# Expert weights in rows of 16 KB: pairs of slots filled by one transfer, and the transposes that match

## The chip, the cores and the metric

The kernel runs on one core of a Trainium2 chip. A core has a matrix engine (PE, TensorE), whose weight loads are shown apart as PEld, and VectorE (DVE), ScalarE (ACT), GpSimd (POOL) and SyncE (SP), each with an instruction stream of its own. They meet at semaphores. Sixteen DMA engines move data between HBM and the on-chip memory SBUF. The metric is the time of one execution on the device, in microseconds, lower is better.

## What is computed

One layer of a hybrid diffusion backbone on 512 latent and 128 context tokens of width 2048, in f32: gated linear attention and windowed attention side by side, a merge, and then the part that matters here, a mixture of 16 experts in which each expert chooses its tokens (64 latent and 16 context ones, 80 rows).

```python
gate, idx = lax.top_k(aff.T, cap)
xs = xf[idx]                                             # 80 rows of 2048
hid = silu(einsum('ecd,edf->ecf', xs, w_gate)) * einsum('ecd,edf->ecf', xs, w_up)
ye = einsum('ecf,efd->ecd', hid, w_down) * gate[..., None]
y = zeros_like(xf).at[idx.reshape(-1)].add(ye.reshape(-1, D))
```

`w_gate` and `w_up` are 2048 x 1024 per expert and `w_down` is 1024 x 2048, 8 MB each: 24 MB per expert, 384 MB in all, each used once.

## The kernel before

The stages up to the router fill the first 60% of the time. After them runs a loop over the experts, with its last round written out because the output work lies in it.

**Pieces and slots.** The weights of an expert come in 24 pieces of 1 MB (128 partitions x 2048 values, 8 KB in each partition): pieces 0 to 7 are `w_gate`, 8 to 15 `w_up`, 16 to 23 `w_down`. Piece j goes to slot j % 8 (`ESLOTS`). Slots 0 and 1 are two of the four slots of the buffer `ring`, slots 2 to 6 lie in `hT`, slot 7 in `ar`. SyncE issues the transfers (`expert`, L623) as each slot comes free: piece j waits until VectorE has finished piece j - 8 (`piece_ready`).

**From piece to product.** ScalarE copies a piece into its high part (fp32r, L1834) and VectorE subtracts to get the low part (L2323). Both lie in one of four split buffers (`SP`), which PE frees (`piece_used`). PE then does three products of high and low parts per tile: 12 matmuls of 512 columns for each piece (L1446 for gate and up, L1471 for down). The tokens are the stationary operand, 80 columns.

**Which row a partition holds.** A product sums over the partitions, so weights and tokens must put the same row of the contraction in the same partition. A gate or up piece covers 256 rows of 4 KB. Partition p gets rows 2p and 2p + 1 of them, 8 KB in one run of HBM. So the tokens' columns that PE transposes for it are every second one, `xs[:, 256 g + 2 p + k]` (L1420 to L1423): the 128 values that one transpose loads as its stationary operand stand 8 bytes apart. A down piece covers 128 rows of 8 KB, one in each partition, and the transposes of the hidden rows (L1430) read 128 adjacent columns.

**Order on PE.** After the 192 gate and up matmuls of an expert come four hidden transposes (L1430), twelve token transposes for the next expert (L1422, k = 0 to 11), four hidden ones, the first down piece, the last four token transposes (k = 12 to 15), and seven more down pieces. Before expert 0 stand sixteen token transposes in three groups, each behind a part of the norm (`norm_xs`, L2326, on VectorE). GpSimd gathers the tokens of the expert after next, adds finished rows into `y`, and in the last round loads and stores the blocks of `y`.

Of the kernel before, what the change touches and what calls it, by code (L numbers as in the profile page):

```python
# [22 lines left out]
ds = bass.ds  # L23

P = 128
D = 2048
# [165 lines left out]
def build(nc, T):  # L192
# [2 lines left out]
    w_a = T["w_branch_a"][0].rearrange("(k p) n -> p k n", p=P)  # L195
    w_b = T["w_branch_b"][0].rearrange("(k p) n -> p k n", p=P)
    w_out = T["w_out"][0].rearrange("(k p) n -> p k n", p=P)
    w_eg = T["w_exp_gate"][0].rearrange("e (g p k) n -> e g p k n", p=P, k=2)
    w_eu = T["w_exp_up"][0].rearrange("e (g p k) n -> e g p k n", p=P, k=2)
    w_ed = T["w_exp_down"][0].rearrange("e (k p) n -> e p k n", p=P)  # L200
    x_lat, x_ctx = T["x_sample"][0], T["x_prompt"][0]
    x_of = [x_lat[t * P:(t + 1) * P, :] for t in range(4)] + [x_ctx]
    x_out = [T["y_sample"][0], T["y_prompt"][0]]
# [10 lines left out]
    with ExitStack() as ctx:  # L214
# [357 lines left out]
        @block.sync  # L572
        def _(sync):
            def load(g, src, dst=None):

                first, turn = g
                s = first % SLOTS

                sync.wait_ge(slot_used, first + turn + 1)
                sync.sem_inc(loads_issued, 1)  # L580
                out = ring[:, s, :] if dst is None else dst(ring[:, s, :])
                sync.dma_start(out, src).then_inc(slot_ready[s], 16)

            def k4(v):
                return v.rearrange("p (k n) -> p k n", k=4)

            def k2(v):
                return v.rearrange("p (k n) -> p k n", k=2)

            for t in range(NT):  # L590
                sync.dma_start(xrow[:, t, :], x_of[t]).then_inc(x_ld[t], 16)
            for q in range(SECTIONS):
                for m in range(2):
                    for j in range(4):
                        cols = slice(m * D + q * BANK, m * D + (q + 1) * BANK)
                        load((G_MOD + 8 * q + 4 * m + j, 0), w_mod[:, 4 * j:4 * j + 4, cols], k4)
                    if m == 0:
                        sync.wait_ge(h_sq, q + 1)
                        sync.dma_start(k4(first_w[:, q, :]), w_in[:, 4 * q:4 * q + 4, 0:BANK]).then_inc(x_ld[q], 16)
            loaded = {"W": 0, "M": 0}  # L600
            for at, (kind, i) in enumerate(CHUNK_ORDER):
                block, j = loaded[kind] // 4, loaded[kind] % 4
                loaded[kind] += 1
                col = (0, BANK, 2 * BANK, 3 * BANK, COL_GR, COL_GR + BANK, COL_SKV, COL_SQ, COL_SQ + BANK)[i]
                if kind == "W":
                    load((G_A + at, 0), w_in[:, 4 * j:4 * j + 4, col:col + BANK], k4)
                else:
                    load((G_A + at, 0), w_mod[:, 4 * j:4 * j + 4, 2 * D + block * BANK:2 * D + (block + 1) * BANK], k4)
            with sync.Fori(0, 4) as n:
                for j in range(12):  # L610
                    w, at = (w_a, w_b)[j // 6], j % 6
                    if at < 4:
                        src = w_in[:, 4 * at:4 * at + 4, ds(n * BANK + (COL_GATE_A, COL_GATE_B)[j // 6], BANK)]
                    else:
                        src = w[:, 4 * (at - 4):4 * (at - 4) + 4, ds(n * BANK, BANK)]
                    load((G_GATE + gate_place(j), n * 24), src, k4)
                    cols = ds(n * BANK + 5 * D, BANK) if j >= 8 else ds(n * (2 * BANK) + (3 * D + j // 4 * BANK), BANK)
                    load((G_GATE + mod_place(j), n * 24), w_mod[:, 4 * (j % 4):4 * (j % 4) + 4, cols], k4)
            with sync.Fori(0, 4) as n:
                for j in range(4):  # L620
                    load((G_OUT + j, n * 4), w_out[:, 4 * j:4 * j + 4, ds(n * BANK, BANK)], k4)

            def expert(e, j):  # L623

                sync.wait_ge(piece_ready, e * EXP_G + (P_EXP + j + 1 - ESLOTS))
                sync.sem_inc(loads_issued, 1)
                at, out = ds(e, 1), exp_slot[j % ESLOTS]
                if j < 16:
                    src = (w_eg, w_eu)[j // 8][at, j % 8, :, :, :].squeeze(0)
                    sync.dma_start(k2(out), src).then_inc(exp_ready[j % ESLOTS], 16)  # L630
                else:
                    sync.dma_start(out, w_ed[at, :, j - 16, :].squeeze(0)).then_inc(exp_ready[j % ESLOTS], 16)

            sync.wait_ge(slot_used, SLOTS + G_OUT + 16)
            for j in range(2):
                expert(0, j)
            sync.wait_ge(piece_used, SP + P_EXP)
            for j in range(2, 5):
                expert(0, j)
            sync.wait_ge(x1_sc, 4 * NT)  # L640
            for j in range(5, 7):
                expert(0, j)
            sync.wait_ge(xs_ld, 16)
            with sync.Fori(0, NE - 1) as e:
                for j in range(7, EXP_G):
                    expert(e, j)
                for j in range(7):
                    expert(e + 1, j)
            for j in range(7, EXP_G):
                expert(NE - 1, j)  # L650


        @block.gpsimd
# [230 lines left out]
        def _(pe):  # L884
# [532 lines left out]

            def xs_transposes(lo, hi, done, bank=0):

                v = xs[0:CAP, 0:D].rearrange("r (g p k) -> r g k p", g=8, k=2)  # L1420
                for k in range(lo, hi):
                    mm = pe.transpose(ps[:, bank + k // 6, (k % 6) * CAP:(k % 6 + 1) * CAP], v[:, k // 2, k % 2, :],  # L1422
                                      ident[0:CAP, 0:CAP])  # L1423
                mm.then_inc(done, 1)

            def hid_transposes(half):

                for k in range(4):
                    col = (4 * half + k) * P
                    mm = pe.transpose(ps[:, 2 + half, k * CAP:(k + 1) * CAP], hid[0:CAP, col:col + P], ident[0:CAP, 0:CAP])  # L1430
                mm.then_inc(hd_tr, 1)

            pe.wait_ge(af_cp, 1)
# [63 lines left out]
        def _(act):  # L1497
# [330 lines left out]
            def split_expert(e, lo, hi):  # L1828

                for j in range(lo, hi):  # L1830
                    s = j % SP
                    act.wait_ge(exp_ready[j % ESLOTS], e * (16 * EXP_G // ESLOTS) + 16 * (j // ESLOTS + 1))
                    act.wait_ge(piece_used, e * EXP_G + (P_EXP + j + 1))
                    act.activation(spE[:, s, 0, :], exp_slot[j % ESLOTS], ACT.Copy).then_inc(piece_high, 1)  # L1834

# [60 lines left out]
        def _(dve):  # L1896
# [429 lines left out]
            def norm_xs(lo, hi):  # L2326
                v = xs[0:CAP, lo:hi]
                dve.scalar_tensor_tensor(v, v, xs[0:CAP, D:D + 1], arows[0:CAP, lo:hi], ALU.mult, ALU.add).then_inc(n2_h, 1)
# [2 lines left out]
            dve.wait_ge(ga_is, 1)  # L2331
            low_expert(0, 0, 2)
            dve.wait_ge(xs_ld, 16)
            norm_xs(0, 768)
            norm_xs(768, 1536)
            norm_xs(1536, D)
            dve.wait_ge(af_cp, 2)
            low_xs(first_xs_parts[:1]).then_inc(xs_l, 1)
# [114 lines left out]
```

## Time and profile before

| | us |
|---|---|
| median of 3 runs | 2909.85 (2909.76 to 2911.56) |
| the profiled execution | 2907.71 |
| its span, first to last instruction | 2905.7 |
| PE busy in it | 2783.0 |
| DVE busy | 2257.8 |
| ACT busy | 1607.0 |

The rows further down come from that one execution. Busy times of engines overlap, so they don't add up to the span; an engine's idle time costs something only where another waits for it.

### The profile page before, as it was taken

How to read it: one execution, taken by the hardware profiler on the slowest of the kernel's cores; microseconds unless marked ns; L12 is line 12 of the kernel's file. 1: busy time of each engine (PE TensorE's matmuls, PEld its weight loads, DVE VectorE, ACT ScalarE, POOL GpSimd, SP SyncE). 2: the span in 40 equal slices, each digit the busy share in tenths (PEclk: the TensorE clock that was granted, in tenths of full speed). 3: DMA queues.
4: the chain of work that ended last, by engine and by line, in shares of the span. 5: the costliest groups of instructions: out<-in, count | busy, mean ns of one | idle time of the engine just before them, and what ended most of it. 6: DMA issues, size and time to landing. Idle time of an engine off the chain costs nothing.

```text
span 2905.7 us, 38120 instructions
## 1 busy us (share of the span) xinstructions
PE 2783.0 (96%) x13699; PEld 2078.4 (72%) x13699; DVE 2257.8 (78%) x2691; ACT 1607.0 (55%) x1977; POOL 305.1 (10%) x206
## 2 busy tenths in 40 slices
PE   6899899999899999999999996999999999999996
PEld 4798658899568888888888884666666666666663
DVE  2465666678878878888775558999998999999987
ACT  4336334444764444434434445777777777777775
POOL 0000000000000000000013000111221112211121
PEclk9999899999999999999999998999999999999998
DMA  9842103333014454454464437999999999999996
GB/s 372 308 131 73 50 19 114 107 120 131 1 61 158 145 178 145 152 172 147 163 254 163 147 119 280 403 402 395 378 388 380 390 385 389 389 385 381 384 377 267
DMA packets 175083, 683.14 MB, mean 235 GB/s; under 512 B 14548, under 2 KB 14756, under 8 KB 119164
## 3 DMA queue, kind: packets, MB, share of 16 engines
q1 hardware_dynamic: 159504, 613.45, 55.8%
q0 software_dynamic: 13392, 67.79, 7.6%
q8 instruction: 76, 1.25, 0.2%
q10 hardware_dynamic: 2064, 0.26, 0.1%
q14 instruction: 47, 0.39, 0.0%
HBM read 649.88 MB, written 31.65 MB: 235 GB/s over the span
## 4 chain that ended last, share of the span: by engine, by line
PE 92%; DVE 4%; ACT 2%; issue 1%; DMA 1%; POOL 0%; DVEq 0%; POOLq 0%; ACTq 0%; SPq 0%
PE ps L960 40%; PE ps L1446 24%; PE ps L1471 12%; PE ps L979 5%; PE ps L986 3%; PE ps L1422 1%; PE ps L1099 1%; PE ps L1250 1%; PE ps L1239 1%; PE ps L1134 1%; PE ps L1220 1%; DMA ring<-w_mod 1%; PE ps L924 1%; DVE ar L2047 0%; ACT ar L490 0%
## 5 line engine op out<-in xcount | busy, mean ns | idle before, releaser
L960 PE MATMUL ps<-split_weights,split_tokens 128*128 128x512 f32 x5040 | 1160.4, 391 | 3.9 <-issue 2.9
L960 PEld LDWEIGHTS ps<-split_weights,split_tokens 128*128 128x128 f32 x5040 | 943.9, 188 | 211.6 <-issue 10.2
L1446 PE MATMUL ps<-split_experts,split_xsT 128*80 128x512 f32 x3072 | 708.9, 392 | 0.0
L531 ACT ACTIVATE split_weights<-ring 128x512 fp32r<-128x512 f32 x384 | 242.9, 633 | 721.7 <-PE ps L960 605.9
L1446 PEld LDWEIGHTS ps<-split_experts,split_xsT 128*80 128x80 f32 x3072 | 454.8, 148 | 251.4 <-issue 1.5
L2323 DVE TENSOR_TENSOR split_experts<-hT,split_experts 128x2048 fp32r<-128x2048 f32 x240 | 540.0, 2284 | 41.2 <-ACT split_experts L1834 41.2
L535 DVE TENSOR_TENSOR split_weights<-ring,split_weights 128x512 fp32r<-128x512 f32 x384 | 266.3, 694 | 362.4 <-ACT split_tokens L532 358.7
L1834 ACT ACTIVATE split_experts<-hT 128x2048 fp32r<-128x2048 f32 x240 | 459.9, 1922 | 123.7 <-PE ps L1446 87.0
L1471 PE MATMUL ps<-split_experts,split_hidT 128*80 128x512 f32 x1536 | 362.3, 395 | 1.6 <-DVE split_experts L2323 1.2
L1471 PEld LDWEIGHTS ps<-split_experts,split_hidT 128*80 128x80 f32 x1536 | 226.7, 149 | 124.4 <-issue 2.5
L2323 DVE TENSOR_TENSOR split_experts<-ring,split_experts 128x2048 fp32r<-128x2048 f32 x96 | 220.0, 2293 | 42.9 <-ACT split_experts L1834 41.9
L538 DVE TENSOR_TENSOR split_tokens<-hT,split_tokens 128x640 fp32r<-128x640 f32 x304 | 249.8, 822 | 0.0
L1834 ACT ACTIVATE split_experts<-ring 128x2048 fp32r<-128x2048 f32 x96 | 184.7, 1925 | 83.1 <-PE ps L1446 51.5
L532 ACT ACTIVATE split_tokens<-hT 128x640 fp32r<-128x640 f32 x304 | 219.9, 723 | 0.0
L424 DVE SCALAR_TENSOR_TENSOR cst<-ring,cond,cst 128x512 f32<-128x512 f32 x300 | 213.0, 745 | 0.6 <-DMA ring<-w_mod 0.6
L979 PE MATMUL ps<-split_tokens,split_weights 128*128 128x384 f32 x768 | 180.6, 344 | 9.6 <-DVE split_tokens L562 9.6
L979 PEld LDWEIGHTS ps<-split_tokens,split_weights 128*128 128x128 f32 x768 | 126.8, 191 | 20.6 <-DVE split_tokens L562 14.3
L986 PE MATMUL ps<-split_tokens,split_weights 128*128 128x256 f32 x768 | 134.9, 285 | 3.0 <-ACT ar L1671 1.8
L833 POOL DMA_INDIRECT y_rows<-ar,sidx x15 | 105.6, 7041 | 279.2 <-DVE ar L2425 262.0
L986 PEld LDWEIGHTS ps<-split_tokens,split_weights 128*128 128x128 f32 x768 | 124.5, 191 | 4.0 <-ACT ar L1671 2.1
L2323 DVE TENSOR_TENSOR split_experts<-ar,split_experts 128x2048 fp32r<-128x2048 f32 x48 | 109.9, 2290 | 13.4 <-ACT split_experts L1834 13.4
L1834 ACT ACTIVATE split_experts<-ar 128x2048 fp32r<-128x2048 f32 x48 | 92.1, 1919 | 31.0 <-PE ps L1446 19.1
(327 smaller groups left out, 2058.3 us busy)
## 6 DMA issues: line engine op xcount, KB each, us to landing
ring<-w_mod SPq DMA_DIRECT2D x96, 1024.0 KB, 5.4
hT<-w_exp_gate SPq DMA_DIRECT2D x80, 1024.0 KB, 7.1
hT<-w_exp_up SPq DMA_DIRECT2D x80, 1024.0 KB, 8.1
hT<-w_exp_down SPq DMA_DIRECT2D x80, 1024.0 KB, 7.8
ring<-w_in SPq DMA_DIRECT2D x64, 1024.0 KB, 5.1
ring<-w_exp_gate SPq DMA_DIRECT2D x32, 1024.0 KB, 7.5
ring<-w_exp_up SPq DMA_DIRECT2D x32, 1024.0 KB, 7.4
ring<-w_exp_down SPq DMA_DIRECT2D x32, 1024.0 KB, 9.9
```

Source lines behind the costliest of these rows:

```text
L424: dve.scalar_tensor_tensor(acc, v, c, acc, ALU.mult, ALU.add).then_inc(z_rd, 1)
L531: self.eng.activation(spW[:, s, 0, :], raw, ACT.Copy)
L532: self.eng.activation(spX[:, s, 0, :], (src[k] if type(src) is dict else src[:, k, :]), ACT.Copy).then_inc(piece_high, 1)
L535: a = self.eng.tensor_tensor(spW[:, s, 1, :], raw, spW[:, s, 0, :].bitcast(F32), ALU.subtract)
L538: self.eng.tensor_tensor(spX[:, s, 1, :], (src[k] if type(src) is dict else src[:, k, :]), spX[:, s, 0, :].bitcast(F32), ALU.subtract).the ...
L960: mm = pe.matmul(ps[:, b, :], spX[:, s, x, b * P:(b + 1) * P], spW[:, s, w, :], start=(k == 0 and x == w), stop=(k == n_k - 1 and x == 1))
L979: mm = pe.matmul(ps[:, c, 0:TA], spW[:, s, w, c * P:(c + 1) * P], spX[:, s, x, 0:TA], start=(k == 0 and x == w), stop=(k == KT - 1 and w = ...
L986: mm = pe.matmul(ps[:, 4 + c // 2, (c % 2) * TB:(c % 2 + 1) * TB], spW[:, s, w, c * P:(c + 1) * P], spX[:, s, x, TA:TOK], start=(k == 0 an ...
L1446: mm = pe.matmul(ps[0:CAP, bank + i, :], xsT[:, x, k, :], spE[:, s, w, col:col + BANK], start=(k == 0 and x == w), stop=(k == KT - 1 and x ...
L1471: return pe.matmul(ps[0:CAP, 4 + n, :], hidT[:, x, k, :], spE[:, (16 + k) % SP, w, n * BANK:(n + 1) * BANK], start=(k == 0 and x == w), st ...
L1834: act.activation(spE[:, s, 0, :], exp_slot[j % ESLOTS], ACT.Copy).then_inc(piece_high, 1)
L2323: dve.tensor_tensor(spE[:, s, 1, :], exp_slot[j % ESLOTS], spE[:, s, 0, :].bitcast(F32), ALU.subtract)\
```

## The change

Slots 0 and 1, 2 and 3, and 4 and 5 are filled in pairs by one transfer of 2 MB; slots 6 and 7 stay alone. In each partition a pair holds one run of 16 KB from HBM: four rows of `w_gate` or `w_up`, or two of `w_down`. The issue waits until the second slot of the pair is free, which is one piece later than the first piece's issue was, and both pieces are there when the one transfer has landed: ScalarE waits on the semaphore of the pair's first slot.

The rows in a partition are others now, so the columns transposed change with them. For k = 0 to 11 the token columns are every fourth one (16 bytes apart), for k = 12 to 15 every second one as before. For the hidden rows, the first six of eight transposes read every second column, the last two adjacent ones. The first group of token transposes before expert 0 needs columns up to 1024, and the three parts of the norm are cut at 1024 and 1536 instead of 768 and 1536. Numbers of matmuls, splits and bytes stay as they are.

```diff
--- before.py
+++ after.py
@@ -195,9 +195,9 @@
     w_a = T["w_branch_a"][0].rearrange("(k p) n -> p k n", p=P)
     w_b = T["w_branch_b"][0].rearrange("(k p) n -> p k n", p=P)
     w_out = T["w_out"][0].rearrange("(k p) n -> p k n", p=P)
-    w_eg = T["w_exp_gate"][0].rearrange("e (g p k) n -> e g p k n", p=P, k=2)
-    w_eu = T["w_exp_up"][0].rearrange("e (g p k) n -> e g p k n", p=P, k=2)
-    w_ed = T["w_exp_down"][0].rearrange("e (k p) n -> e p k n", p=P)
+    w_eg = T["w_exp_gate"][0]
+    w_eu = T["w_exp_up"][0]
+    w_ed = T["w_exp_down"][0]
     x_lat, x_ctx = T["x_sample"][0], T["x_prompt"][0]
     x_of = [x_lat[t * P:(t + 1) * P, :] for t in range(4)] + [x_ctx]
     x_out = [T["y_sample"][0], T["y_prompt"][0]]
@@ -622,32 +622,34 @@
 
             def expert(e, j):
 
-                sync.wait_ge(piece_ready, e * EXP_G + (P_EXP + j + 1 - ESLOTS))
+                sync.wait_ge(piece_ready, e * EXP_G + (P_EXP + j + (2 if j % ESLOTS < 6 else 1) - ESLOTS))
                 sync.sem_inc(loads_issued, 1)
-                at, out = ds(e, 1), exp_slot[j % ESLOTS]
-                if j < 16:
-                    src = (w_eg, w_eu)[j // 8][at, j % 8, :, :, :].squeeze(0)
-                    sync.dma_start(k2(out), src).then_inc(exp_ready[j % ESLOTS], 16)
-                else:
-                    sync.dma_start(out, w_ed[at, :, j - 16, :].squeeze(0)).then_inc(exp_ready[j % ESLOTS], 16)
+                at, slot = ds(e, 1), j % ESLOTS
+                two = slot < 6
+                assert not (two and slot % 2)
+                out = (ring[:, 0:2, :].rearrange("p s n -> p (s n)") if slot == 0 else hT_area((slot - 2) * SLOT, 2 * SLOT)) if two else exp_slot[slot]
+                w, rows, per = ((w_eg, w_eu)[j // 8], 2 * P, 2) if j < 16 else (w_ed, P, 1)
+                lo, n = slot * rows, 2 if two else 1
+                src = w[at, lo:lo + n * rows, :].squeeze(0).rearrange("(p k) n -> p k n", k=n * per)
+                sync.dma_start(out.rearrange("p (k n) -> p k n", k=n * per), src).then_inc(exp_ready[slot], 16)
 
             sync.wait_ge(slot_used, SLOTS + G_OUT + 16)
-            for j in range(2):
-                expert(0, j)
+            def experts(e, lo, hi):
+
+                for j in range(lo, hi):
+                    if j % ESLOTS not in (1, 3, 5):
+                        expert(e, j)
+
+            experts(0, 0, 2)
             sync.wait_ge(piece_used, SP + P_EXP)
-            for j in range(2, 5):
-                expert(0, j)
+            experts(0, 2, 4)
             sync.wait_ge(x1_sc, 4 * NT)
-            for j in range(5, 7):
-                expert(0, j)
+            experts(0, 4, 7)
             sync.wait_ge(xs_ld, 16)
             with sync.Fori(0, NE - 1) as e:
-                for j in range(7, EXP_G):
-                    expert(e, j)
-                for j in range(7):
-                    expert(e + 1, j)
-            for j in range(7, EXP_G):
-                expert(NE - 1, j)
+                experts(e, 7, EXP_G)
+                experts(e + 1, 0, 7)
+            experts(NE - 1, 7, EXP_G)
 
 
         @block.gpsimd
@@ -1417,17 +1419,21 @@
 
             def xs_transposes(lo, hi, done, bank=0):
 
-                v = xs[0:CAP, 0:D].rearrange("r (g p k) -> r g k p", g=8, k=2)
+                four = xs[0:CAP, 0:3 * 4 * P].rearrange("r (g p k) -> r g k p", g=3, k=4)
+                two = xs[0:CAP, 3 * 4 * P:D].rearrange("r (g p k) -> r g k p", g=2, k=2)
                 for k in range(lo, hi):
-                    mm = pe.transpose(ps[:, bank + k // 6, (k % 6) * CAP:(k % 6 + 1) * CAP], v[:, k // 2, k % 2, :],
+                    column = four[:, k // 4, k % 4, :] if k < 12 else two[:, k // 2 - 6, k % 2, :]
+                    mm = pe.transpose(ps[:, bank + k // 6, (k % 6) * CAP:(k % 6 + 1) * CAP], column,
                                       ident[0:CAP, 0:CAP])
                 mm.then_inc(done, 1)
 
             def hid_transposes(half):
 
                 for k in range(4):
-                    col = (4 * half + k) * P
-                    mm = pe.transpose(ps[:, 2 + half, k * CAP:(k + 1) * CAP], hid[0:CAP, col:col + P], ident[0:CAP, 0:CAP])
+                    at = 4 * half + k
+                    pair = hid[0:CAP, at // 2 * 2 * P:(at // 2 + 1) * 2 * P].rearrange("r (p k) -> r k p", k=2)
+                    rows = pair[:, at % 2, :] if at < 6 else hid[0:CAP, at * P:(at + 1) * P]
+                    mm = pe.transpose(ps[:, 2 + half, k * CAP:(k + 1) * CAP], rows, ident[0:CAP, 0:CAP])
                 mm.then_inc(hd_tr, 1)
 
             pe.wait_ge(af_cp, 1)
@@ -1829,7 +1835,7 @@
 
                 for j in range(lo, hi):
                     s = j % SP
-                    act.wait_ge(exp_ready[j % ESLOTS], e * (16 * EXP_G // ESLOTS) + 16 * (j // ESLOTS + 1))
+                    act.wait_ge(exp_ready[(0, 0, 2, 2, 4, 4, 6, 7)[j % ESLOTS]], e * (16 * EXP_G // ESLOTS) + 16 * (j // ESLOTS + 1))
                     act.wait_ge(piece_used, e * EXP_G + (P_EXP + j + 1))
                     act.activation(spE[:, s, 0, :], exp_slot[j % ESLOTS], ACT.Copy).then_inc(piece_high, 1)
 
@@ -2331,8 +2337,8 @@
             dve.wait_ge(ga_is, 1)
             low_expert(0, 0, 2)
             dve.wait_ge(xs_ld, 16)
-            norm_xs(0, 768)
-            norm_xs(768, 1536)
+            norm_xs(0, 1024)
+            norm_xs(1024, 1536)
             norm_xs(1536, D)
             dve.wait_ge(af_cp, 2)
             low_xs(first_xs_parts[:1]).then_inc(xs_l, 1)
```

SyncE's instructions from the end of the stage before to the second transfer of the loop's body, before and after (a row is a line of the kernel, the operation, what it writes and reads, and values per partition):

```order
-L630 DMA ring<-w_exp_gate 128x2048 x2
-L630 DMA hT<-w_exp_gate 128x2048 x5
-L644 UNCONDITIONAL_BRANCH
-L644 ISA
-L630 ISA
-L630 DMA ar<-w_exp_gate 128x2048
+L634 DMA ring<-w_exp_gate 128x4096
+L634 DMA hT<-w_exp_gate 128x4096 x2
+L634 DMA hT<-w_exp_gate 128x2048
+L649 UNCONDITIONAL_BRANCH
+L649 ISA
+L634 ISA
```

Seven transfers ahead of the loop have become four, and inside it each `ring` pair and each of the two `hT` pairs is one transfer of 4096 values per partition.

VectorE before the loop over the experts, first before and then after:

```order
L2323 TENSOR_TENSOR split_experts<-ring,split_experts 128x2048 x2
L2328 SCALAR_TENSOR_TENSOR ar<-ar,cst 80x768 x2
L2328 SCALAR_TENSOR_TENSOR ar<-ar,cst 80x512
L2304 TENSOR_TENSOR split_xsT<-ps,split_xsT 128x480
L2323 TENSOR_TENSOR split_experts<-hT,split_experts 128x2048
```

```order
L2329 TENSOR_TENSOR split_experts<-ring,split_experts 128x2048 x2
L2334 SCALAR_TENSOR_TENSOR ar<-ar,cst 80x1024
L2334 SCALAR_TENSOR_TENSOR ar<-ar,cst 80x512 x2
L2310 TENSOR_TENSOR split_xsT<-ps,split_xsT 128x480
L2329 TENSOR_TENSOR split_experts<-hT,split_experts 128x2048
```

The first part of the norm has grown from 768 to 1024 columns and the second has shrunk to 512; nothing else moved. On PE the order and number of instructions are the same in both, and only the steps inside the transposes differ.

## Rows read from the trace of the kernel before

**Rows 1.** the page: busy time of each engine; DMA share in 40 slices, in tenths
```profile
PE 2783.0 (96%) x13699; PEld 2078.4 (72%) x13699; DVE 2257.8 (78%) x2691; ACT 1607.0 (55%) x1977; POOL 305.1 (10%) x206
...
DMA  9842103333014454454464437999999999999996
```

**Rows 2.** table of stretches, 1800 to 2800 us: busy us (count) by engine, PEclk, DMA share, GB/s
```profile
1800.00:2800.00 1000.00, 1000.00 (x4557) 657.30 (x4556) 906.77 (x484) 752.65 (x469) 190.93 (x57) 1.00 1.00 389
```

**Rows 3.** chain of waits, one expert: start us, us, what
```profile
1846.48 44.05 PE ps L1446 x192
1890.54 0.28 PE ps L1430 x4
1890.82 1.44 PE ps L1422 x12
1892.26 0.28 PE ps L1430 x4
1892.53 2.79 PE ps L1471 x12
...
1895.76 19.29 PE ps L1471 x84
```

**Rows 4.** waits, 1800 to 2800 us: total us, times, longest us
```profile
SPq L626 <- DVE split_experts L2323: 779.8, 350, 4.1
...
ACT split_experts L1834 <- PE ps L1446: 142.7, 188, 0.9
```

**Rows 5.** DMA issues at 1782 to 1783 us: count, KB each, median us to landing
```profile
hT<-w_exp_up SPq DMA_DIRECT2D x1, 1024.0 KB, 17.3
```

**Rows 6.** timeline around pieces 10 and 11 of expert 0: start us, us, engine, line
```profile
1782.53 0.33 SPq L630 DMA_DIRECT2D hT<-w_exp_up  x1
...
1797.24 1.93 ACT L1834 ACTIVATE split_experts<-hT 128x2048 fp32r<-128x2048 f32 x1 [0.85 <-PE ps L1446]
1799.97 1.93 ACT L1834 ACTIVATE split_experts<-hT 128x2048 fp32r<-128x2048 f32 x1 [0.80 <-PE ps L1446]
...
1800.89 6.69 DVE L2323 TENSOR_TENSOR split_experts<-hT,split_experts 128x2048 fp32r<-128x2048 f32 x3
```

**Rows 7.** chain of waits where expert 0 starts
```profile
1772.75 0.94 DVE ar L2328
...
1773.82 2.45 PE ps L1422 x16
```

**Rows 8.** DMA queues and issues, 2000 to 2068 us: packets, MB, share; then as rows 5
```profile
q1 hardware_dynamic: 3470, 25.28, 92.2%
q0 software_dynamic: 171, 1.14, 7.1%
...
hT<-w_exp_up SPq DMA_DIRECT2D x5, 1024.0 KB, 7.0
...
ring<-w_exp_down SPq DMA_DIRECT2D x2, 1024.0 KB, 10.0
```

**Rows 9.** groups of weight loads (PEld) by line, 1734 to 2906 us: busy us, mean ns
```profile
L1422 PEld LDWEIGHTS ps<-cst,ar 80*128 80x128 f32 x256 | 34.4, 214 | 10.5 <-issue 8.5
L1430 PEld LDWEIGHTS ps<-cst,ar 80*128 80x128 f32 x128 | 12.8, 146 | 7.2 <-DVE ar L2310 4.4 <-issue 0.2
L1353 PEld LDWEIGHTS ps<-cst,ar 128*128 128x128 f32 x77 | 8.4, 141 | 1.7 <-issue 1.7
```

**Rows 10.** chain of waits, contiguous 128x128 transposes of the router stage
```profile
1739.44 2.33 PE ps L1353 x20
```

**Rows 11.** table of stretches where expert 0 starts
```profile
1773.00:1777.00 4.00, 3.15 (x18) 2.74 (x19) 3.75 (x5) 1.79 (x4) 0.56 (x1) 0.50 0.62 172
```

**Rows 12.** DMA issues of 2825 to 2850 us, the second block of y
```profile
cst<-y_rows POOLq DMA_DIRECT2D x1, 1024.0 KB, 14.2
```

**Rows 13.** timeline of the same block: its issue, and its squares on ScalarE
```profile
2830.06 0.60 POOL L853 DMA_DIRECT2D cst<-y_rows  x1
...
2846.67 1.86 ACT L1851 ACTIVATE ps<-cst 128x2048 f32<-128x2048 f32 x1
```

## Prediction

> **What bounds the kernel now.** I read the page first. The matrix engine (PE) is busy for 96% of the span, and from slice 25 of 40 the DMA line shows nines as well [rows 1]. The change touches the expert stage alone, so I asked for a table of its steady part: from 1800 to 2800 us PE is busy for 1000.00 of 1000.00 us, at the full granted clock, while the DMA engines show a share of 1.00 at 389 GB/s [rows 2]. Two resources at their limit call for the chain of waits, which says which one paces. The chain repeats one block per expert: 44.05 us of gate and up products, hidden transposes of 0.28 us, twelve token transposes of 1.44 us, again 0.28 us, then down products of 2.79 us and, with four more token transposes between, of 19.29 us. They end at 1915.05, 68.57 us after 1846.48 [rows 3]. Everything in it is PE. The waits agree: ScalarE's split waits for PE, 142.7 us in 188 waits for its gate and up products, and a landing stands nowhere in the list, and the queue that issues the weights waits for VectorE to free a slot, 779.8 us in 350 waits [rows 4]. So DMA is busy and yet early; PE paces. A nanosecond put on PE between experts is paid in full, and one saved on a transfer is worth nothing unless it becomes late.
>
> **The change, part by part.**
> *The transfers.* Six of eight slots come as three 2 MB transfers, so an expert issues 15 instead of 24. The bytes stay. Fewer issues gain nothing, for the issuing queue only waits [rows 4]. What changes is when data are there: a pair needs both its slots free, so it is issued when its second half used to be, and its first half counts as landed only with the second. The tight place is expert 0, where other loads share the engines. Its piece 11 was issued at 1782.53 and landed 17.3 us later, at 1799.83; its split began at 1799.97, and that of piece 10 at 1797.24 [rows 5, 6]. Now 10 and 11 come together, and as the engines have a backlog the pair ends about where piece 11 did. The split of piece 10 then starts some 2.6 us late, at 1799.9, and ends near 1801.8. VectorE took piece 10 from 1800.89 on, three pieces in 6.69 us [rows 6]; it would start at 1801.8 and end at 1804.1. PE takes a piece in 44.05/16 = 2.75 us [rows 3], and in expert 0, by the end of the transposes before it at 1773.82 + 2.45 = 1776.27 [rows 7] and its first products at the lower clock, it needs piece 10 at about 1805. It is covered by about 1 us. The engines may also run dry while they wait for the later issue, up to 2.7 us (one piece). The bounds are 0 and 2.7 us, once; I take 0.5. In the steady part a piece has more room: medians of issue to landing are 7 to 10 us [rows 8], against 17.4 us between the issue and the split of piece 11 in expert 0 [rows 6], the time that eight slots give; a pair costs its first half one piece (2.75 us) and one more megabyte (about 2.6 us at 403 GB/s, below), which leaves over 1 us in the worst case of 10.
>
> *Twelve token transposes per expert.* Columns k = 0 to 11 were picked out of rows of the gathered tokens with a step of two elements, now with a step of four. The step is in the stationary operand: the weight load reads 128 values 8 bytes apart, now 16. What does a step cost? The hidden transposes have the same shape and step one, and four take 0.28 us, 70 ns each; twelve with step two take 1.44 us, 120 ns each [rows 3]. The weight loads show the same: a mean of 214 ns against 146 ns, and 141 ns for the contiguous transposes L1353 [rows 9]. Is the 70 ns the load at all? Twenty contiguous 128x128 transposes take 2.33 us, 116 ns each or 0.91 ns per moving column [rows 10]; times 80 columns that is 73 ns. So contiguous transposes are set by their moving side and the load hides in at most 70 ns, whereas with step two the load itself is the limit at 120 ns. For step four the trace has no row. Below, nothing: if all that counts is that neighbours are not adjacent, it stays at 120 ns. (Less than nothing would need the load to speed up with distance; the least would be 70 ns, -50 ns each, -9 us in all, and no row hints at it.) Above: if the load pays for the distance that it covers, 1024 bytes in 120 ns, then 2048 bytes take 240 ns, and 512 bytes would take 60 ns, which fits under the 70. In between: each doubling adds the same, 50 ns. I take 240, as the law of distance is the one that fits both known points without an extra assumption: +120 ns x 12 x 15 = +21.6 us. Nothing covers it; the transposes stand in the chain one behind the other [rows 3].
>
> The Trainium skill has a rule against this change: SBUF — State Buffer (SBUF: two separate sides; the note on cachelines stands under Door 1, the DMA port swizzle) says that SBUF works in 16-byte lines and wants at least two hits in a line for full bandwidth. Step two has two hits, step four has one. Taken literally, step two should be free, yet the trace shows it at 120 against 70 ns; taken as a price per line it is the doubling above. No run so far shows step four.
>
> *Six hidden transposes per expert* go from step one to step two, which the trace has priced: 120 - 70 = 50 ns, x 6 x 16 = +4.8 us [rows 3].
>
> *The start of expert 0.* The first norm covers 1024 instead of 768 columns: 0.94 us [rows 7] x 1024/768 = 1.25 us, +0.3 us before the first transpose; the later norms end as before. The sixteen transposes there take 2.45 us, 153 ns each [rows 7], at a granted clock of 0.50, the level of 1.2 GHz [rows 11]; twelve at 240 instead add 12 x 87 ns = +1.0 us. Together +1.3 us.
>
> *The last expert.* Rows of y are loaded beside the weights, by another queue. The second block of them is issued at 2830.06 and takes 14.2 us to land, and ScalarE squares it at 2846.67, 2.4 us later [rows 12, 13]. If the queues take turns by transfers' rows, rows of 16 KB leave the other queue a third instead of a half. The first y comes beside slots 6 and 7, which stay at 8 KB; the second could be late by a few us. Bounds 0 and 3 us; I take 0.3.
>
> **Sum** against the profiled execution (2907.71 us, span 2905.7): 21.6 + 4.8 + 1.3 + 0.5 + 0.3 = +28.5 us, 2936.2. The median of the runs, 2909.85, lies 2.1 above that execution, so the same sum gives 2938.3; I say 2938.
>
> **The rivals.**
> A. *The distance costs nothing more* (on the other side: not slower beyond what can be told). The point that decides is whether a weight load with step four still takes 120 ns. For it: a price for leaving adjacency explains 70 to 120 as well. Then the sum is 4.8 + 0.3 + 0.5 + 0.3 = +5.9, 2915.8; without the stall and the tail +5.1, 2915.0.
> B. *Each doubling of the step adds 50 ns*: 12 x 15 x 50 ns = 9.0, with 0.2 at the start, + 5.9 = +15.1, 2925.
> C. *Transfers of 16 KB rows are slower and DMA paces.* In 68 us the weight queue moved 25.28 MB at 92.2% of the share, 25.28/(0.922 x 68) = 403 GB/s, beside 7.1% of the other queue [rows 8]. 24 MB pieces (25.17 MB) take 62.5 us, with the other queue 67.3 of 68.57. If the rows ran 10% slower: 68.7 + 4.8 = 73.5 us per expert, +5 x 15 = +75 us, 2985; at 5% slower PE, itself slower by 1.7 us, still hides it. [...]
> D. *Larger rows move faster and something gains.* In the steady part no engine waits for a landing [rows 4], so nothing there can be had. It would have to come from expert 0 and the tail, 1 to 3 us, and only beside A or cheaper transposes.
>
> **How the numbers follow.** Forecast 50%, with its own range of 2931 to 2943; A 22%; B 16%; C 6%; D with cheaper transposes 6%. What a measurement here can tell from no change is about 0.2%, 5.8 us, so 2904 to 2915.7. A lies on that edge: I count half of it as the same. Same: 11 + 2 = 13%; faster 4%; slower 83%. The range from 2914 to 2943 holds A, B and the forecast, and leaves out C and D and a little of each end.
>
> **What would show it.** The group of token transposes in the profile after, as mean of a weight load in the steady part (214 ns now: near 330 with the forecast, near 214 with A) and as the pieces of twelve in the chain (1.44 us now: 2.9, 1.44 or 2.0); hidden transposes at 0.48 and 0.38 us for the 0.28s; an expert of 68.57 + 0.30 + 1.44 = 70.3 us. PE still busy 100% of the steady part. ScalarE's split waiting for a landing, or PE idle in it, would prove the transfers late; a mean rate that falls more than 389 x 68.57/70.3 = 379 GB/s together with such waits would be C. I am wrong if twelve transposes take 1.5 us, or if PE idles between pieces.

## The result: slower by 8.6 us, a third of what was forecast

| | before | after |
|---|---|---|
| median of the runs, us | 2909.09 (8 runs, 2907.24 to 2911.56) | 2917.72 (8 runs, 2915.36 to 2919.82) |
| the profiled execution, its span | 2907.71, 2905.7 | 2919.82, 2917.8 |

The ratio is 1.0030, with a 95% interval of 1.0021 to 1.0038. The change is slower, as forecast, and inside the range of 2914 to 2943; but 2938 was forecast, and its own range, from 2931, is missed by 13 us. The result lies 2 us above rival A (2915 to 2915.8).

The two profiled executions differ by 12.1 us, more than the medians. Expert 0's first product starts at 1780.64 in after's and at 1776.30 in before's, and only 0.27 us of these 4.3 is the longer norm. The kernels e2, e3, e6 and e7 below have after's code up to there and start at 1778.3 to 1780.7, and e1 has before's and starts at 1777.9. So the execution decides most of what lies ahead, and I measure from that start on.

The first product of each expert in the trace gives three stretches. In the experiments they tell one cost from another, which a total of 2900 us can't. Before and after are one profiled execution each:

| us | expert 0 | a period of experts 1 to 14 | start of expert 15 to the end | all |
|---|---|---|---|---|
| before | 70.02 | 68.567 | 99.40 | 1129.36 |
| after | 70.70 | 68.827 | 102.89 | 1137.17 |
| difference | +0.68 | +0.26, x 14 = +3.64 | +3.49 | +7.81 |

**The chain of waits** of after, first where expert 0 starts and then one expert of the steady part (start us, us, what). L1426, L1436, L1452, L1477, L2334 are L1422, L1430, L1446, L1471, L2328 of before:

```profile
1776.82 1.21 DVE ar L2334
...
1778.16 2.38 PE ps L1426 x16
...
1780.64 46.08 PE ps L1452 x192
...
1851.50 44.06 PE ps L1452 x192
1895.56 0.43 PE ps L1436 x4
1895.99 1.44 PE ps L1426 x12
1897.43 0.38 PE ps L1436 x4
1897.81 2.79 PE ps L1477 x12
1900.60 0.43 PE ps L1426 x4
1901.03 19.30 PE ps L1477 x84
```

Against [rows 3] one piece kept its time that I had expected to double: the twelve token transposes, 1.44 us with a step of four as with a step of two. The hidden ones went from 0.28 and 0.28 to 0.43 and 0.38, +0.25 us. The sixteen transposes before expert 0 take 2.38 us, not more than the 2.45 of [rows 7], and the norm before them 1.21 for 0.94.

**The weight loads** between 1900 and 2800 us say the same (line, operation, operands, count, busy us, mean ns, idle before):

```profile
L1426 PEld LDWEIGHTS ps<-cst,ar 80*128 80x128 f32 x212 | 28.8, 215 | 1.8
L1436 PEld LDWEIGHTS ps<-cst,ar 80*128 80x128 f32 x104 | 14.3, 195 | 1.6
```

Token loads: 215 ns, a mean over twelve with a step of four and four with a step of two, where [rows 9] had 214 (and 330 was forecast). Hidden loads: 195 for 146 (142 in before between 1900 and 2800 us), a mean over six with a step of two and two adjacent ones.

**The table of stretches** for 1800 to 2800 us, columns as in [rows 2]:

```profile
1800.00:2800.00 1000.00, 1000.00 (x4541) 659.42 (x4540) 903.34 (x483) 749.55 (x468) 189.78 (x57) 1.00 0.98 386
```

PE is as full as before. The rate fell from 389 to 386 GB/s, as a longer expert makes it (389 x 68.57/68.83 = 387.5), so rival C has no footing in the steady part.

**The last expert** is where a new wait stands. First ScalarE's waits in 2800 to 2920 us (total us, times, longest), then the chain of the same stretch; L1857 squares a block of y (L1851 of before), L1840 splits a weight piece:

```profile
ACT ps L1857 <- DMA cst<-y_rows: 2.6, 1, 2.6
...
ACT ps L1857 <- DMA ar<-y_rows: 1.3, 1, 1.3
```

```profile
2819.66 19.14 DMA y_rows<-ar,sidx
2838.84 0.57 issue
2839.41 0.60 POOL ar L855
2840.01 19.41 DMA cst<-y_rows
2859.44 2.01 ACT ps L1857 x2
2861.58 0.09 issue
2861.68 1.90 ACT split_experts L1840
```

Before, ScalarE had neither wait, and the second block of y took 14.2 us and was there 2.4 us early [rows 12, 13]. Now it takes 19.4, with its issue 1.3 us later against the start of the expert (25.10 for 23.80 us). The later issue comes from the transfer ahead, which scatters expert 14's rows into y: 19.1 us for 17.8. Together that is 6.5 us more, less 2.4 of slack: 4.1 us of lateness, which ScalarE pays as 1.3 for the first block and 2.6 for the second. The split of a weight piece is queued behind each square, and PE waits for the splits. Which queue took the bandwidth is seen in the tables of queues while that block was on its way, of before (2831 to 2844 us) and then of after (2841 to 2859): packets, MB, share of the 16 engines. q1 carries the weights, q0 the rows of y.

```profile
q1 hardware_dynamic: 438, 3.15, 58.4%
q0 software_dynamic: 316, 2.33, 43.9%
```

```profile
q1 hardware_dynamic: 418, 5.45, 72.6%
q0 software_dynamic: 303, 2.22, 29.9%
```

The packets stand at 1.4 to 1 both times, but q1's have grown from 7.2 to 13.0 KB on the mean (3.15 MB/438, 5.45/418), so that q0 needs 18 us for what it got in 13.

### The profile page after: what moved, and what is told of

The parts are those of the page before. It is cut to its first block, busy times and chain, and to the rows that moved or that the text cites. A ratio compares the mean times of both kernels' runs of the same rounds, so it can differ in the third digit from the quotient of the medians.

```text
span 2917.8 us, 37472 instructions
## 1 busy us (share of the span) xinstructions
PE 2792.3 (96%) x13699; PEld 2086.1 (71%) x13699; DVE 2257.1 (77%) x2691; ACT 1607.0 (55%) x1977; POOL 302.6 (10%) x206
## 4 chain that ended last, share of the span: by engine, by line
PE 91%; DVE 3%; ACT 2%; DMA 2%; issue 1%; POOL 0%; DVEq 0%; POOLq 0%; ACTq 0%; SPq 0%
PE ps L962 39%; PE ps L1452 23%; PE ps L1477 12%; PE ps L981 5%; PE ps L988 3%; PE ps L1426 1%; PE ps L1252 1%; PE ps L1241 1%; PE ps L1101 1%; PE ps L926 1%; PE ps L1222 1%; PE ps L1136 1%; DMA cst<-y_rows 1%; DMA y_rows<-ar,sidx 1%; ACT ar L490 0%
## 5 line engine op out<-in xcount | busy, mean ns | idle before, releaser
L1452 PE MATMUL ps<-split_experts,split_xsT 128*80 128x512 f32 x3072 | 709.4, 392 | 0.1
L1452 PEld LDWEIGHTS ps<-split_experts,split_xsT 128*80 128x80 f32 x3072 | 455.1, 148 | 251.6 <-issue 1.9
L1840 ACT ACTIVATE split_experts<-hT 128x2048 fp32r<-128x2048 f32 x240 | 460.1, 1924 | 125.5 <-PE ps L1452 84.2
L1477 PE MATMUL ps<-split_experts,split_hidT 128*80 128x512 f32 x1536 | 362.3, 395 | 1.7 <-DVE split_experts L2329 1.2
L1477 PEld LDWEIGHTS ps<-split_experts,split_hidT 128*80 128x80 f32 x1536 | 226.7, 149 | 124.4 <-issue 2.5
L1840 ACT ACTIVATE split_experts<-ring 128x2048 fp32r<-128x2048 f32 x96 | 184.7, 1925 | 84.9 <-PE ps L1452 51.1
L1840 ACT ACTIVATE split_experts<-ar 128x2048 fp32r<-128x2048 f32 x48 | 92.1, 1918 | 30.6 <-PE ps L1452 18.7
## 6 DMA issues: line engine op xcount, KB each, us to landing
hT<-w_exp_up SPq DMA_DIRECT2D x32, 2048.0 KB, 12.1
```

Source lines behind the costliest of these rows:

```text
L1452: mm = pe.matmul(ps[0:CAP, bank + i, :], xsT[:, x, k, :], spE[:, s, w, col:col + BANK], start=(k == 0 and x == w), stop=(k == KT - 1 and x ...
L1477: return pe.matmul(ps[0:CAP, 4 + n, :], hidT[:, x, k, :], spE[:, (16 + k) % SP, w, n * BANK:(n + 1) * BANK], start=(k == 0 and x == w), st ...
```

## The experiments

Three questions were open: why twelve transposes with a step of four cost nothing, what the rest is made of, and which part of the change made y late.

**1. Hidden transposes adjacent again (e2).** The kernel after, with

```diff
-                    rows = pair[:, at % 2, :] if at < 6 else hid[0:CAP, at * P:(at + 1) * P]
+                    rows = hid[0:CAP, at * P:(at + 1) * P]
```

so that the down products sum rows that don't belong together.

> The changed kernel, with the hidden transposes back to adjacent columns (the down products then sum wrong pairs of rows; times alone count). Theory 1, a step of two costs 50 ns per transpose and a step of four costs no more than that: the expert's period falls from 68.83 to 68.57 us, the four hidden transposes from 0.43 to 0.28 us in the chain, and the run takes 2917.7 - 16 x 0.26 = 2913.5, still 4.5 us above the kernel before, all of it in expert 0 and in the last expert. Rival, the loss in the loop comes from the transfers and not from the transposes: the period stays at 68.8 and the time at 2917.7.

Measured: 2912.90 (11 runs; ratio to before 1.0011, 1.0002 to 1.0020). Its chain:

```profile
1894.40 0.28 PE ps L1436 x4
1894.68 1.44 PE ps L1426 x12
1896.12 0.28 PE ps L1436 x4
1896.39 2.79 PE ps L1477 x12
```

The period is 68.560, before's own. So the hidden transposes are the whole of the 0.26 us an expert, and the token transposes with a step of four are nothing of it. ScalarE still waits 2.2 and 1.0 us for y, and the last stretch takes 102.49: the second loss is another.

**2. One step for each four transposes (e1).** Before, but in the loop the token transposes read adjacent columns for k = 0 to 3 (L1427), every fourth for 4 to 7 (L1429), every eighth for 8 to 11 (L1431) and every sixteenth for 12 to 15 (L1433). The columns are then the wrong ones for the weights.

```diff
+                    elif k < 4:
+                        mm = pe.transpose(out, xs[0:CAP, k * P:(k + 1) * P], ident[0:CAP, 0:CAP])
+                    elif k < 8:
+                        mm = pe.transpose(out, view(4)[:, k // 4, k % 4, :], ident[0:CAP, 0:CAP])
+                    elif k < 12:
+                        mm = pe.transpose(out, view(8)[:, k // 8, k % 8, :], ident[0:CAP, 0:CAP])
+                    else:
+                        mm = pe.transpose(out, view(16)[:, 0, k, :], ident[0:CAP, 0:CAP])
```

> The kernel before, with the token transposes inside the loop reading their stationary operand with other steps, each form on a line of its own: k = 0 to 3 adjacent columns, 4 to 7 a step of 4, 8 to 11 of 8, 12 to 15 of 16 (the tokens' columns no longer match the weights' rows; times alone count). Theory 1, a step costs once and its size costs nothing: weight loads near 146 ns on the first line and near 214 ns on the other three, transposes 70 and 120 ns apart, four of step 16 in 0.43 us. Rival, the price grows from a larger distance on (a step of 8 or 16, 32 and 64 bytes): the loads of step 8 or 16 well above 214 ns, four of step 16 in 0.9 us or more.

One run, 2904.04, so I read its trace and not its time, the chain first, then the weight loads of 1830 to 2800 us:

```profile
1892.19 0.28 PE ps L1427 x4
1892.46 0.48 PE ps L1429 x4
1892.94 0.45 PE ps L1431 x4
...
1896.46 0.40 PE ps L1433 x4
```

```profile
L1440 PEld LDWEIGHTS ps<-cst,ar 80*128 80x128 f32 x112 | 11.0, 142 | 2.4
L1433 PEld LDWEIGHTS ps<-cst,ar 80*128 80x128 f32 x56 | 8.5, 198 | 1.7
L1429 PEld LDWEIGHTS ps<-cst,ar 80*128 80x128 f32 x56 | 7.8, 216 | 0.0
L1431 PEld LDWEIGHTS ps<-cst,ar 80*128 80x128 f32 x56 | 7.6, 208 | 0.0
L1427 PEld LDWEIGHTS ps<-cst,ar 80*128 80x128 f32 x56 | 4.9, 140 | 0.0
```

Adjacent 140 ns; steps of 4, 8 and 16 elements 216, 208, 198 ns. The price is for leaving adjacency, once, and a step four times as long costs nothing more, if anything less. Both the forecast's law of distance and rival B's 50 ns a doubling are refuted.

**3. The last expert's pairs in halves (e3).** The kernel after, but from piece 8 of the last expert on each pair goes as two transfers of 1 MB in rows of 8 KB, issued together, and ScalarE waits for each half by itself.

```diff
+                if halves and two:
+                    for h in range(2):
+                        sync.dma_start(out[:, h * per:(h + 1) * per, :], src[:, h * per:(h + 1) * per, :])\
+                            .then_inc(exp_ready[slot + h], 16)
+                    return
```

> The changed kernel, with the pairs of the last expert from its piece 8 on issued as two transfers of 1 MB each, every one of them in rows of 8 KB (the rows of a pair stay where they are in a partition), each half with a semaphore of its own. Theory 1, rows of 16 KB take two thirds of the DMA engines from the queue that loads y: the two blocks of y land within about 15 us of their issue instead of 19.4, ScalarE no longer waits 1.3 and 2.6 us for them, and the time is 2917.7 - 3.6 = 2914.1. Rival, the y blocks are late because pairs are issued later and two at once: the issue times are the same here, so they are late as before and the time stays at 2917.7.

Measured: 2915.12 (11 runs; 1.0014, 1.0005 to 1.0023), 2.6 us less than after. The second y block landed in 14.5 us, ScalarE no longer waits for y, and the last stretch is 100.17, 0.8 us over before's. ScalarE waits instead for landings of down pieces, 0.8 us at the longest:

```profile
ACT split_experts L1849 <- DMA hT<-w_exp_down: 1.7, 3, 0.8
...
ACT split_experts L1849 <- DMA ring<-w_exp_down: 0.8, 1, 0.8
ACT split_experts L1849 <- DMA ar<-w_exp_down: 0.8, 1, 0.8
```

This fits long rows as the cause, but it took away two things at once: the row's size, and a piece's wait for its pair's second megabyte.

**4. Pairs, but rows of 8 KB (e5).** Before, with the change's pairs, issues and waits, and each pair as two runs of 8 KB per partition; every transpose is as before.

```diff
+                    lo = slot * 2 * P
+                    src = w[at, lo:lo + n * 2 * P, :].squeeze(0).rearrange("(g p k) n -> p g (k n)", g=n, k=2)
...
+                    lo = slot * P
+                    src = T["w_exp_down"][0][at, lo:lo + n * P, :].squeeze(0).rearrange("(g p) n -> p g n", g=n)
```

> The kernel before with slots filled in pairs by one transfer of 2 MB, but in rows of 8 KB in both halves, and all transposes as before: pairing alone, without long rows. Theory 1, only row size and steps cost: the period is 68.57 us, ScalarE does not wait for y, and the time is that of the kernel before, 2909.1, plus up to 0.5 in expert 0. Rival, pairing itself costs (half the loss or more): 2912.7 or above, with ScalarE waiting for y, or for weights in expert 0.

Measured: 2912.48 (11 runs; 1.0010, 1.0001 to 1.0020). The period is 68.567 as before, but the last stretch is 102.34, nearly after's. ScalarE's timeline there (start us, us, engine, line, operation; in brackets the idle time and what ended it):

```profile
2851.57 1.92 ACT L1843 ACTIVATE split_experts<-ring 128x2048 fp32r<-128x2048 f32 x1 [3.10 <-DMA ring<-w_exp_down]
2853.39 1.86 ACT L1860 ACTIVATE ps<-cst 128x2048 f32<-128x2048 f32 x1
```

and the transfers issued in 2820 to 2850 us:

```profile
ring<-w_exp_down SPq DMA_DIRECT2D x1, 2048.0 KB, 20.7
```

Here y comes in time (15.1 us), and the first down piece, 16, is 3.1 us late: it waits for the second half of its pair, 20.7 us after the issue. "The row's size alone" falls. With short rows the weights take 60.9% of the engines while y is loaded (2834 to 2848 us; 58.4% before) and the pair is late itself; with long rows they take 72.6% and y is late. About 3 us are lost either way.

**5. Only the down pairs, or only the others, in halves (e6, e7).** The kernel after with the edit of experiment 3 for pieces 16 to 21 of the last expert (e6), or for its pieces 8 to 13 (e7).

```diff
-            experts(NE - 1, 7, EXP_G)
+            experts(NE - 1, 7, 16)
+            experts(NE - 1, 16, EXP_G, True)
```

> The changed kernel, with only the down pairs of the last expert (pieces 16 to 21) issued as two transfers of 1 MB in rows of 8 KB, each half with its own semaphore; pieces 8 to 13 of it stay pairs of 16 KB rows. Theory 3, the last expert is late because piece 16 cannot start before piece 17 has landed too, one megabyte more that the engines must move beside the blocks of y: splitting these pairs brings back most of the loss, and from the start of the last expert to the end of the span it takes 100.2 us as in the run with all halves (102.9 in the changed kernel, 99.4 before), 2915. Rival, it is the rows of 16 KB of the pairs in flight earlier, 8 to 13, that hold up the scatter of expert 14 and the first block of y: 102 us or more stay.

> The counterpart: only pieces 8 to 13 of the last expert as halves, the down pairs left as one transfer of 2 MB each. Theory 3: nothing comes back, 102.5 to 103 us from the start of the last expert to the end, 2917.7, and ScalarE waits for the second block of y or for piece 16. Rival: it comes back here, 100 to 101 us.

Measured: e6 2914.22 (11 runs; 1.0016, 1.0007 to 1.0025), e7 2917.42 (11 runs; 1.0026, 1.0017 to 1.0035), after 2917.72. With the down pairs halved ScalarE waits for no landing at all and the last stretch is 99.54, nearly before's 99.40; the y blocks land in 9.9 and 14.7 us. The rows are then 8 KB, as in e5, and both halves are issued where the pair was, but piece 16 no longer waits for piece 17. So it is that wait which made it late in e5. With the up pairs halved these waits remain:

```profile
ACT ps L1867 <- DMA cst<-y_rows: 2.1, 1, 2.1
...
ACT ps L1867 <- DMA ar<-y_rows: 0.3, 1, 0.3
```

The first block took 12.0 us and the second 19.0, as in after. In e7's one profiled execution the last stretch is 100.85, 2.0 us shorter than after's, where 102.5 to 103 was expected. Its waits for y are 1.5 us shorter in all (2.4 for 3.9), as y was issued 24.0 us into the expert instead of 25.1, and its first 84 down matmuls took 21.15 us for 21.79. But over its 11 runs the median recovers only 0.3 us. The pairs of down pieces carry the loss of the last expert; whether the up pairs add to it stays open.

**6. Pairs for gate and up only (e8).** If the account holds, the change without its down part costs nothing.

```diff
-                two = slot < 6
+                two = slot < 6 and j < 16
...
-                    rows = pair[:, at % 2, :] if at < 6 else hid[0:CAP, at * P:(at + 1) * P]
+                    rows = hid[0:CAP, at * P:(at + 1) * P]
```

> The kernel after, with rows of 16 KB and pairs for gate and up alone; the down pieces come as eight single transfers in 8 KB rows, and the transposes of the hidden rows read adjacent columns again. Theory: what the change costs hangs on the down weights (the hidden transposes with a step between columns, 0.26 us an expert, and the last expert's down pairs beside the rows of y, about 3.5 us). Then the period of experts 1 to 14 is 68.57 us as before, the stretch from the start of expert 15 to the end is about 99.5 us as before (99.40), ScalarE waits nowhere for rows of y, and only some 0.5 us in expert 0 is left: 2909.5 to 2910 us, no change from before (2909.1). Rival: rows of 16 KB for gate and up cost something too (they take bandwidth from what runs beside them, or the step of the token transposes costs after all): 2912 us or more.

Measured: 2910.31 (11 runs) beside 2908.97; the ratio is 1.0005, 0.9996 to 1.0014. Its stretches are 70.06, 68.560 and 99.41, before's to 0.04 us, with all token transposes as in after. No wait for y, which took 15.2 us and was used without a pause. Two thirds of the change (12 of its 18 paired pieces) cost nothing in the trace, and win nothing; by the interval of the medians a cost of up to 4 us stays possible.

**7. The other direction: two rows of 4 KB (e4).** If adjacency is what counts, before pays it too, for its sixteen token transposes. This kernel is before, but a gate or up piece gives partition p the rows p and p + 128 of its 256, so that all transposes read adjacent columns and each partition's 8 KB come from two places in HBM.

```diff
-    w_eg = T["w_exp_gate"][0].rearrange("e (g p k) n -> e g p k n", p=P, k=2)
-    w_eu = T["w_exp_up"][0].rearrange("e (g p k) n -> e g p k n", p=P, k=2)
+    w_eg = T["w_exp_gate"][0].rearrange("e (g k p) n -> e g p k n", p=P, k=2)
+    w_eu = T["w_exp_up"][0].rearrange("e (g k p) n -> e g p k n", p=P, k=2)
...
-                v = xs[0:CAP, 0:D].rearrange("r (g p k) -> r g k p", g=8, k=2)
+                v = xs[0:CAP, 0:D].rearrange("r (g k p) -> r g k p", g=8, k=2)
```

> The kernel before with the step taken out: gate and up pieces in two rows of 4 KB per partition that are 128 rows apart, and token transposes of adjacent columns. Theory 1, each of the 16 token transposes of an expert falls from 120 to about 70 ns and the loads still keep up: 16 x 50 ns x 15 = 12 us less, and 0 to 1 at the start, so 2897; the period is 67.8 us. Rival, rows of 4 KB are slower in the DMA engines and the loads become the pace: 24 MB at less than 371 GB/s shows as ScalarE waiting for landings and a period above 68.57 us, a time above 2909.

Measured: 2900.40 (5 runs, 2897.94 to 2901.30), ratio 0.9965, 0.9951 to 0.9978: 9 us faster than before and 17 us faster than after, the best of the study. Its chain and its table of stretches:

```profile
1892.64 0.28 PE ps L1430 x4
1892.92 0.83 PE ps L1422 x12
1893.74 0.28 PE ps L1430 x4
1894.02 0.04 issue
1894.06 3.00 PE ps L1471 x12
1897.05 0.28 PE ps L1422 x4
1897.33 19.30 PE ps L1471 x84
```

```profile
1800.00:2800.00 1000.00, 999.46 (x4592) 651.16 (x4591) 912.44 (x487) 758.14 (x472) 224.79 (x57) 1.00 1.02 392
```

The transposes fell from 1.44 + 0.43 to 0.83 + 0.28 us, 0.76 an expert, but the first down piece rose from 2.79 to 3.00 and 0.04 of idle came before it, so the period fell by 0.52, to 68.05 for the 67.8 expected. By the timeline the twelve matmuls take 3.00 us in both kernels; before, they start 0.2 us under the transposes ahead of them, and here 0.04 behind. The chain says only "issue". One of PE's waits in the kernel at this place is for the low part of the hidden rows (L2315 on VectorE); in e4's timeline that operation ends at 1893.91 and the first of the down piece's weight loads starts at 1894.03, 0.12 us later. In before's last expert, where the chain names this wait, the distance is 0.14. So the part of the 0.76 that was not gained is most likely held by VectorE, though no run moves it. Half as long rows gave 392 GB/s, and ScalarE waits for no landing in the steady part.

Not all of the 9 us is this. The period and the start account for 7.8 (0.52 x 14 and 0.46 in expert 0, 69.56 for 70.02); the other 1.2 lies in the last expert (98.23 for 99.40), where e4 transposes no tokens. The first 84 down matmuls took 21.90 us there in before and 20.90 in e4, and in the 12 us from 48 us into that expert the mean granted clock was 0.72 in before and 0.86 in e4. e1, whose last expert is before's own, has the same 0.86 and took 98.01.

## Why the forecast came out wrong

- **The token transposes, +21.6 us: the step that failed.** It said that "the load pays for the distance that it covers". Measured: +0, with 1.44 us for twelve before and after instead of 2.9, and in experiment 2 loads of 216, 208 and 198 ns for steps of 4, 8 and 16. I had two points, 70 and 120 ns, and took the law that fits both "without an extra assumption". It did need one: that 60 ns hides under the 70. A price for not being adjacent needed none and fitted as well; that was rival A. Cache lines of 16 bytes, drawn in from the Trainium skill (SBUF — State Buffer, Door 1: the DMA port swizzle), gave the law a mechanism that this load doesn't show: two hits a line are not free (step two, 214 ns against 142), and one hit a line (step four, 216) or one in four lines (step sixteen, 198) costs no more. Why leaving adjacency costs 50 ns a transpose stays open.
- **The hidden transposes, +4.8 us: right.** 0.25 to 0.26 us an expert instead of 0.30, 4.2 us in all, as four in a row cost 0.43 rather than 0.48. Experiment 1 took the 0.26 out again, and its median is 4.8 us below after's.
- **The start of expert 0, +1.3 us: 0.3.** The norm grew by 0.27 for the 0.3 forecast; the 1.0 for transposes fell with the first point.
- **The stall in expert 0, +0.5 us (0 to 2.7): none.** The pairs are later as worked out: ScalarE's waits of 1770 to 2800 us now hold landings, where before has none.

```profile
ACT split_experts L1840 <- DMA hT<-w_exp_up: 3.5, 2, 2.3
ACT split_experts L1840 <- DMA hT<-w_exp_down: 1.2, 1, 1.2
```

  PE's chain has no gap from it, so the cover of about 1 us held. Expert 0 took 70.70 for 70.02; 0.26 of it is the hidden transposes, and the 0.4 left is the granted clock. The tables of its first 10 us, of before and then of after:

```profile
1776.30:1786.30 10.00, 10.00 (x38) 6.30 (x39) 8.51 (x6) 7.56 (x7) 4.58 (x5) 0.85 1.02 372
1780.64:1790.64 10.00, 10.00 (x36) 6.29 (x37) 8.10 (x6) 7.42 (x5) 4.64 (x5) 0.80 0.99 310
```

  A mean clock of 0.85 is worth 1.5 us less of work in 10, one of 0.80 is worth 2.0. The kernels e3, e6 and e7 have after's code in this expert: they took 70.06, 70.75 and 71.28 us at 0.87, 0.80 and 0.74. Less the clock's part and the 0.26, all four are at 68.4 to 68.5, and so is before without the 0.26. The stall does show in e5, the pairs in rows of 8 KB: 70.44 us at 0.87, which leaves 69.1, 0.6 more than in the others, and there the chain runs over the landing of an up pair (16.52 us from 1790.79).

- **The last expert, +0.3 us (0 to 3): mis-sized, 3.5, beyond its own bounds.** The mechanism was written down (queues that take turns by rows, y's share falling from a half to a third) and then priced at nearly nothing, with the thought that the first block comes beside slots 6 and 7. It had been read off one block and its 2.4 us of slack, without pair 16/17, which is in flight beside both. And the pair's own lateness, which the other half of the argument knew from expert 0, wasn't applied here (experiment 4).
- **Rivals.** A, at 22%, had the transposes right; its 5.9 us fall short of the 8.6 by the last expert. That its total came within 2 us is in part luck, for it holds 0.5 for a stall that did not come and 0.3 for what cost 3.5. B fell in experiment 2, C in the table of stretches, and D found nothing: rows of 16 KB won nowhere. That the result lies inside the range of 2914 to 2943 is owed to A's having been let into it.
- **The account.** Norm 0.3, hidden transposes 0.26 x 16 = 4.2, last expert 3.5 less the 0.26 of it that was just counted, expert 0's granted clock 0.4: 8.1 us against 8.6 by the medians. The 0.4 belongs to the one execution profiled, not to the change.

## What to carry to other kernels

When PE paces, lay out the weights so that the small operand is transposed from adjacent columns, and let the DMA rows get shorter for it: here the rows of 4 KB fed PE as well as those of 8 or 16, and that gave 7.8 of the 9 us gained. Making a transfer larger makes its first half wait for its second; here that was free where landings had slack and was paid at the end, where another queue shared the engines. So look at a change's transfers there and not only in the steady part. And when two laws fit the two points a trace has, don't choose by taste: put the sum between them or give both the same chance.

## What the runs showed of the hardware

- The load of an f32 operand of 80 partitions and 128 columns took 140 to 142 ns when its columns were adjacent and 198 to 216 when they weren't (before, after, e1, e4); a step of 16 elements was the cheapest of those with a step. The trace doesn't say why.
- While the second block of y was loaded, the two queues kept their ratio of packets and not of bytes: 438 packets to 316 in before and 418 to 303 in after, while the weights' share of the bytes rose from 57% to 71%. In this case the queue with the longer rows took bandwidth from the other.
- A transfer of 2 MB beside the loads of y took 20.7 us in rows of 8 KB and 15.3 in rows of 16 KB (the pair 16/17 in e5 and in after), and the second y block then took 15.1 and 19.4: what one gained the other lost.
- In the steady part the rates were 389 GB/s with rows of 8 KB, 386 with three quarters of the bytes in rows of 16, and 392 with two thirds of the bytes in rows of 4, each as fast as PE asked for it; none of these shows what the rows could do alone.
- The granted clock differs between executions of the same code: over the first 10 us of expert 0 its mean was 0.80, 0.87, 0.80 and 0.74 in after, e3, e6 and e7, and the expert's time differed by 1.2 us with it.
